# One weight cast moved ahead of the hidden rows' cast in the expert loop of a one-core decoder step

## The reference, cut to what matters

```
def expert_block(args):
    xb, e = args
    hid = jax.nn.silu(xb @ w_gate[e]) * (xb @ w_up[e])
    return hid @ w_down[e]

yb = lax.map(expert_block, (x_pad, block_e)).reshape(P, D)
```

## Time and profile before

| | |
|---|---|
| median of 3 runs | 2644.43 us |
| the profiled execution | 2653.36 us, its span 2651.7 us |
| TensorE busy | 2367.6 us, 89% of the span |
| VectorE, ScalarE busy | 1381.6 us (52%), 1048.1 us (40%) |
| expert loop, layer 0 | from about 807 to 1283 us |
| expert loop, layer 1 | from about 2144 to 2576 us |
| mean granted TensorE clock | 0.916 of full speed |

### The profile page before, as it was taken

The page is one execution under the profiler, slowest core; times in us unless marked ns, Lnnn a source line. Parts: engine busy times, 40 slices in busy tenths (PEclk is TensorE's granted clock), DMA queues, the critical chain, the costliest instruction groups (busy, mean ns, idle before and its releaser), DMA issues. The chain is left out here.

```text
span 2651.7 us, 39920 instructions
## 1 busy us (share of the span) xinstructions
PE 2367.6 (89%) x11761; PEld 1769.1 (67%) x11761; DVE 1381.6 (52%) x2288; ACT 1048.1 (40%) x1771; POOL 313.2 (12%) x394
## 2 busy tenths in 40 slices
PE   2999999786958999999698999999989779999976
PEld 0876666565847888888377765666658658888851
DVE  2412310455876765756285244333348768755657
ACT  1211130443124655655252334344341137655655
POOL 1000000452001010110010224100000011111003
PEclk7899999677978999999798899999989879999995
DMA  7156653745135876876554445332323259867856
GB/s 266 48 180 208 218 204 135 206 143 191 57 124 199 313 256 234 319 255 244 186 168 159 133 152 169 125 109 91 96 109 119 92 180 352 323 225 250 295 213 216
DMA packets 193772, 501.45 MB, mean 189 GB/s; under 512 B 19364, under 2 KB 39301, under 8 KB 187176
## 3 DMA queue, kind: packets, MB, share of 16 engines
q1 hardware_dynamic: 165080, 404.85, 44.3%
q0 software_dynamic: 19056, 66.20, 7.0%
q10 hardware_dynamic: 9536, 29.13, 2.9%
HBM read 434.51 MB, written 68.77 MB: 190 GB/s over the span
## 5 line engine op out<-in xcount | busy, mean ns | idle before, releaser
L1817 DVE TENSOR_TENSOR e_wl<-e_raw,e_wh 128x1024 fp32r<-128x1024 f32 x384 | 450.9, 1220 | 105.7 <-ACT e_wh L1729 105.3
L1729 ACT CAST e_wh<-e_raw 128x1024 fp32r<-128x1024 f32 x384 | 379.3, 1047 | 68.8 <-DMA e_raw<-in_e_gate 21.4
L1648 PE MATMUL e_psG<-e_wh,e_xh 128*128 128x512 f32 x784 | 321.9, 411 | 10.2 <-issue 7.4
L1650 PE MATMUL e_psG<-e_wh,e_xl 128*128 128x512 f32 x784 | 312.3, 398 | 0.0
L1649 PE MATMUL e_psG<-e_wl,e_xh 128*128 128x512 f32 x784 | 310.9, 397 | 0.0
L1648 PEld LDWEIGHTS e_psG<-e_wh,e_xh 128*128 128x128 f32 x784 | 149.1, 190 | 42.9 <-issue 8.3
L519 PE MATMUL in_ps<-in_w_upper,in_h_upper 128*128 128x512 f32 (+1 forms) x432 | 177.0, 410 | 0.0
L1650 PEld LDWEIGHTS e_psG<-e_wh,e_xl 128*128 128x128 f32 x784 | 148.6, 189 | 37.0
L520 PE MATMUL in_ps<-in_w_lower,in_h_upper 128*128 128x512 f32 (+1 forms) x432 | 171.5, 397 | 0.0
L1649 PEld LDWEIGHTS e_psG<-e_wl,e_xh 128*128 128x128 f32 x784 | 149.4, 191 | 32.0
L521 PE MATMUL in_ps<-in_w_upper,in_h_lower 128*128 128x512 f32 (+1 forms) x432 | 170.7, 395 | 0.0
(11 more groups left out here) (538 smaller groups left out, 4408.6 us busy)
## 6 DMA issues: line engine op xcount, KB each, us to landing
e_raw<-in_e_gate SPq DMA_DIRECT2D x32, 2048.0 KB
e_raw<-in_e_up SPq DMA_DIRECT2D x32, 2048.0 KB
e_raw<-in_e_down SPq DMA_DIRECT2D x32, 2048.0 KB
x<-in_ada_w SPq DMA_DIRECT2D x40, 1024.0 KB, 5.3
yrows<-e_y ACTq DMA_DIRECT2D x49, 512.0 KB, 7.0
x<-in_cache SPq DMA_DIRECT2D x64, 320.0 KB, 3.3
a_pages<-in_cache SPq DMA_DIRECT2D x64, 320.0 KB, 3.5
in_w_raw<-in_a_w_in POOLq DMA_DIRECT2D x48, 256.0 KB, 4.5
```

The lines of the kernel that those rows point to most:

```text
L1648: T.matmul(out, upper[:, k, :], wh[:, z, cols], start=k == 0, stop=False)
L1650: mm = T.matmul(out, lower[:, k, :], wh[:, z, cols], start=False, stop=k == PIECES * n - 1)
L1729: S.copy(wh[:, z, c * PC:(c + 1) * PC], raw[:, z, c * PC:(c + 1) * PC]).then_inc(s_hi[z], 1)
L1817: V.tensor_tensor(wl[:, z, at], raw[:, z, at], wh[:, z, at].bitcast(F32), ALU.subtract).then_inc(s_lo[z], 1)
```

## The change

In ScalarE's program for a slot, the branch that casts the first two pieces of the next slot's `up` weights is split in two. The first piece is now cast ahead of `copy_hidden`, the second stays behind it. The number of casts is the same; there is one branch more in each slot.

```diff
@@ -1768,8 +1768,9 @@
                 act.wait_ge(s_used[UP], b + 1)
                 copy_x(1)
                 renew(DOWN, b, now, b + 1, range(2, PIECES))
+                renew(UP, b + 1, soon, b + 1, range(1))
                 copy_hidden(b)
-                renew(UP, b + 1, soon, b + 1, range(2))
+                renew(UP, b + 1, soon, b + 1, range(1, 2))
                 silu(b + 1)
                 renew(UP, b + 1, soon, b + 1, range(2, PIECES))
```

## The result

The changed kernel takes 2678.28 us (median of 4 runs, 2669.67 to 2682.63), the kernel before 2648.89 (4 runs, 2643.95 to 2659.81). The ratio is 1.0111, 95% interval 1.0086 to 1.0137: **slower by 29 us**. The forecast was slower by 15.7 us, 2660 (2648 to 2669): the side and the place were right, the size was half of what was measured, and the time lies above the range. The forecast stood on the median of three runs, 2644.43; with the fourth run the median before is 4.5 us higher, so of the 18 us between 2660 and 2678.28 some 14 are the change's own.

What follows compares the result with a forecast made beforehand. TensorE, never waiting in the loop's 18.11 us slots, was taken as the bound. Late slots 13.3, borderline 0.3 and carry to following slots 2.1 sum to 15.7 us, put on the 2644.43 median: 2660 us, range 2648 to 2669.

Steps and rivals of the forecast that it cites:

- w + 0.30: TensorE's loss ahead of down in a late slot; w is ScalarE's present wait for up; 0.81 us in the slot shown.
- 16 early slots: Fresh-up slots with the load issued 13.8 us ahead of the turn: landing 2.1 ahead of the hidden cast, no cost.
- twelve late slots: Slots where ScalarE already waits for up, 9.7 us in all; at present lateness predicted to cost 13.3 us.
- two borderline ones: Slots with nil wait whose up cast started as soon as ScalarE was free; each 0 to 0.3 us, 0.3 together.
- signs of being wrong: No TensorE wait on psY, waits in slots whose load comes early, or a lower granted clock.
- followers: Six late slots after a late or borderline one: relief -5.7 us, later down issue +7.8, net +2.1.
- Rival 4: A gain from earlier casts letting VectorE and the loads start earlier, not exceeding noise; chance 0.02.
- rival 1: Absorbed: TensorE's pauses let transfers catch up, cost 0 to 10 us, 2644 to 2655; chance 0.25.
- 1.3 per slot reaches the landing: Of the 2.2 us later down issue, 0.9 is absorbed by backlog; 1.3 delays the next up, six slots, +7.8 us.
- estimate of 18 to 19 us: Total cost if the 2.0 us fixed transfer cost holds, 0.5 less being absorbed in each of six slots.
- rival 2: Full carry: the whole down-issue delay goes through, follow-on slots stall 2.5 each, 22 us, 2666; chance 0.11.
- rival 3: The clock falls after each of 13 stalls, 20 us on top of 15.7, 2680; chance 0.04.

Runs made afterwards that it cites:

- experiment 2: Changed kernel with only the wait for the up load and a one-column copy ahead of the hidden cast, both pieces behind; ratio 1.007 to the kernel before.
- experiment 9: The changed kernel, unaltered, executed and profiled once more (its second execution): 2680.78 us.
- experiment 8: Kernel before with five or eight extra ScalarE copies ahead of copy_hidden, no wait for a load: 1.0169 with five, 2791 us (single run) with eight.
- experiment 5: Changed kernel loading only half of each down weight in the loop: both layers 1.0057 (one slot more in layer 1); second run, layer 1 alone, 1.0039.
- experiment 3: Changed kernel with VectorE's fourth down piece ahead of the lower part of the hidden rows: 1.002 against the kernel before.

## Why the prediction was half right

**What held.** TensorE has nothing to gain in the loop. The slack of the hidden cast is 1.24 us. A first late slot waits w + 0.30: the predicted 0.81 of the slot shown is 0.83, though that close it is luck, since w differs between executions (the slot waits 0.70 in the second one), and the other first slots are up to 0.5 off. The 16 early slots are untouched, the extra branch is free. The waits are where they were forecast: the twelve late slots and the two borderline ones, of which the second is the slot before the last of layer 1. Of the signs of being wrong one came, a lower granted clock; and the followers' waits pass the 2.5 us that was named as the upper end. Rival 4, a gain, did not come; rival 1, absorbed, is refuted by the followers.

**The step that failed first: "I take 0.9, a bit under the middle; 1.3 per slot reaches the landing".** Nothing was absorbed. SyncE's issues of `down` and `up`, and the casts behind them, in the changed kernel (ScalarE's row of the second cast stands above, 934.02):

```profile
916.65 0.37 SPq L1573 DMA_DIRECT2D e_raw<-in_e_down  x1
921.19 0.38 SPq L1573 DMA_DIRECT2D e_raw<-in_e_up  x1
```

```profile
913.09 1.05 ACT L1729 CAST e_wh<-e_raw 128x1024 fp32r<-128x1024 f32 x1 [2.37 <-DMA e_raw<-in_e_up]
```

The issue of `down` comes 3.56 behind the first weight cast (the forecast had 3.55), and the `up` of the next slot is cast 17.37 behind that issue. In the kernel before the same distance was 938.37 - 921.07 = 17.30. For all 13 casts of the changed kernel behind which TensorE waited it is 17.2 to 18.2, in the 12 late ones of before 16.6 to 18.0. For the six followers alone the mean went from 17.1 to 17.6, so a later issue is a later landing by at least as much. The backlog in front of `down` did shrink, but the queue then ran thin elsewhere. From the issue of `down` to the cast, the follower of before moved at 357 GB/s and that of the changed kernel at 310:

```profile
921.07:938.37 17.30, 17.30 (x82) 14.11 (x81) 15.74 (x16) 13.42 (x18) 1.44 (x2) 1.00 0.94 357
```

```profile
916.65:934.02 17.37, 17.12 (x80) 13.61 (x78) 14.38 (x14) 11.13 (x15) 3.65 (x2) 1.00 0.89 310
```

That is 6.2 MB and 5.4 MB. The means over the six followers are 6.4 and 5.6: 0.8 MB less ahead of the landing, which at 400 GB/s would be 2.0 us, and no time saved. DMA share and GB/s of the changed kernel, us by us, behind the issue of `down` and behind the end of its transfer:

```profile
917.00:918.00 1.00, 1.00 (x6) 0.82 (x5) 1.00 (x2) 0.94 (x1) 0.00 (x0) 1.00 0.39 109
918.00:919.00 1.00, 1.00 (x5) 0.77 (x5) 1.00 (x2) 0.54 (x1) 0.00 (x0) 1.00 1.20 266
...
923.00:924.00 1.00, 1.00 (x6) 0.81 (x5) 1.00 (x2) 0.32 (x1) 1.00 (x1) 1.00 1.24 277
924.00:925.00 1.00, 1.00 (x6) 0.79 (x5) 1.00 (x2) 0.00 (x0) 1.00 (x1) 1.00 0.62 139
```

All six followers of the changed kernel have the first dip, in the 3 us behind the issue of `down` (102 to 319 GB/s, us by us), and a second one 7 to 9 us behind it (98 to 260 at the lowest). In the followers of before, with a transfer in flight ahead of the next, the rate in the same places is never under 323. That the second is the start of `up` is read from these rows and not tested. The six followers were put at 10.2 us with the borderline slots' share; they took 16.4. The Trainium skill (DMA: Bandwidth & Descriptors, Anatomy of one DMA) with its fixed cost of about 2.0 us, which that section measures on GpSimd's path and not on SyncE's, pointed to less absorption, the right way, but the estimate of 18 to 19 us worked out from it would have been short as well.

**Smaller: the first late slots** were put at 5.5 us and took 7.1, mostly one borderline slot, put at up to 0.3, that waited 1.16; in the second execution it waited 0.64. That a load lands just in time in one execution says little for the next.

**The step that failed second: the clock** had a chance of 0.04 and stood as an all-or-nothing rival with 20 us. It is a partial one: about 8.5 us in one execution, 5 in the full slots of the other. The argument against it, "mostly under 2 us", was right for waits under 2 us; it fell with the first step, since the followers' waits without absorption are 2.5 to 3.3, but for one of 1.46. Full carry (rival 2, 22 us) and part of rival 3 together are the result: 23.5 + 8.5. They were held to be apart from each other, and one causes the other.

## What to carry to other kernels

An engine that executes in order passes a wait on to all that stands behind it: before moving an instruction forward, ask what it waits for, not how long it takes, and put instructions whose data may be late behind those on which the bound engine hangs. If the wait also delays the next issue of loads on a queue that is almost full, count that delay in full in the next turn of the loop: what looked like backlog here was a distance that repeated itself, from one issue to a landing. And add the clock to any forecast in which TensorE's waits reach 2 us: here the shortest wait with a fall was 2.0 (experiment 2), the longest without one 3.2 (experiment 9).

## What the runs showed of the hardware

- In dense 128x512 work, waits of TensorE of 1.18 and 1.46 us (28 and 16 of them, experiment 8) never brought the granted clock down; of 29 waits of 3.15 us, 14 did. Between, of 2.0 to 2.7 us, some did (2.00, 2.23 and 2.41 in experiment 2) and some did not (2.43 and 2.63 in the second run of experiment 5). A fall mostly lasted 3.4 us at 0.50 and cost 1.55 to 1.7 us. In the changed kernel four of the five falls began 0.05 to 1.2 us after TensorE had gone on, the fifth 0.3 before.
- Landing of the 2 MB load of `up`, issued 4.5 to 5.2 us behind that of `down` on one queue: 17.2 to 18.2 us after the issue of `down` in the changed kernel, 16.6 to 18.0 before, whether `gate` was 3.8 or 1.8 us from landing at that issue (924.89 - 921.07 before; in the changed kernel `gate` was cast at 918.46 and `down` issued at 916.65). With `up` issued 8.4 behind (experiment 3) it was 19.0 to 19.8.
- The loops repeat between executions to 0.1 us (452.8 and 380.4) as long as no load is late enough to reach TensorE; the start of the first loop moved by 13 us.
